# Prompt and memory attention between the K slabs, gates and memory caches between the V slabs: one decoder step on one core

## The reference

```python
q_sb, k_sb, v_sb, q_mem, p_rw, g_sb, g_mem, g_rw = _split(x @ w_in, IN_SPLITS)
o_sb = sb_mix(sb_heads(q_sb), k_sb, v_sb, sb_bias)        # stick-breaking attention, 8 heads of 64
o_mem = _mem_attend(q_mem..., mem_k, mem_v)               # softmax over 256 memory tokens, 4 heads of 128
o_rw, shift, wkv = _rwkv7(p_rw, ...)                      # a recurrence over the tokens, 8 heads of 64
merged = (jax.nn.sigmoid(g_sb) * (o_sb @ w_sb_o) + jax.nn.sigmoid(g_mem) * (o_mem @ w_mem_o)
          + jax.nn.sigmoid(g_rw) * (o_rw @ w_rw_o))
h = _layer_norm(DN_ALPHA * x + merged @ w_out, ln1_g, ln1_b)
y = _layer_norm(DN_ALPHA * h + _moe(h, ...), ln2_g, ln2_b)  # top 4 of 32 experts
```

## Time and profile before

| | us |
|---|---|
| median of 3 runs | 1773.66 |
| lowest, highest | 1770.39, 1776.94 |
| the profiled execution | 1772.1 |
| its span, first to last instruction | 1770.5 |
| TensorE busy | 1546.1 |
| VectorE busy | 596.5 |
| ScalarE busy | 278.0 |
| HBM read in MB | 528.65 |

### The profile page before, as it was taken

The page is one execution under the profiler, slowest core; times in us unless marked ns, Lnnn a source line. Parts: engine busy times, 40 slices in busy tenths (PEclk is TensorE's granted clock), DMA queues, the critical chain, the costliest instruction groups (busy, mean ns, idle before and its releaser), DMA issues.

```text
span 1770.5 us, 20938 instructions
## 1 busy us (share of the span) xinstructions
PE 1546.1 (87%) x7762; PEld 827.2 (47%) x7762; DVE 596.5 (34%) x888; ACT 278.0 (16%) x538; POOL 179.9 (10%) x285
## 2 busy tenths in 40 slices
PE   7976777768889997789999999999999999999992
PEld 5865534446777774444334343433343334334341
DVE  1699633157544445421212121111212121212125
ACT  1100233103311111201011101110111111011102
POOL 5422132102032112000000000000000000000000
PEclk9997878889989998889999999999999999999997
DMA  8798687765311105449999999999999999999970
GB/s 299 245 333 305 233 288 268 255 247 156 103 18 48 48 1 210 162 206 391 430 413 410 414 427 412 410 422 419 412 412 424 417 412 411 429 412 411 413 306 25
DMA packets 83769, 533.84 MB, mean 302 GB/s; under 512 B 8591, under 2 KB 9674, under 8 KB 59106
## 3 DMA queue, kind: packets, MB, share of 16 engines
q1 hardware_dynamic: 69714, 487.61, 68.1%
q0 software_dynamic: 14000, 45.53, 7.8%
HBM read 528.65 MB, written 4.46 MB: 301 GB/s over the span
## 4 chain that ended last, share of the span: by engine, by line
PE 78%; DVE 8%; issue 5%; ACT 4%; DMA 4%; POOL 1%; SPq 1%; POOLq 0%; DVEq 0%; ACTq 0%
PE bank L723 75%; PE bank L724 2%; DMA ring<-in_w_in 2%; ACT memT L1537 1%; ACT projT L1522 1%; DVE ring L1591 1%; DMA ring<-in_w_mem_kv 1%; DVE ring L1680 1%; DVE arena L1682 0%; DMA ring<-in_cache_sb_k 0%; DVE arena L1797 0%; DVE arena L1799 0%; DVE arena L1798 0%; ACT arena L1342 0%; DVE arena L2028 0%
## 5 line engine op out<-in xcount | busy, mean ns | idle before, releaser
L723 PE MATMUL bank<-arena 128*128 128x128 f32 (+9 forms) x2172 | 363.7, 357 | 38.0 <-DVE arena L1799 13.3
L723 PEld LDWEIGHTS bank<-arena 128*128 128x128 f32 (+3 forms) x2172 | 244.1, 184 | 165.2 <-issue 137.0
L723 PE MATMUL bank<-ring,memT 128*64 128x512 f32 (+2 forms) x1152 | 279.3, 598 | 43.3 <-ACT memT L1537 42.2
L723 PE MATMUL bank<-projT,ring 128*128 128x264 f32 x1056 | 265.1, 408 | 29.8 <-DMA ring<-in_w_in 20.9
L1968 DVE TENSOR_SCALAR arena<-bank 128x256 f32<-128x256 f32 x64 | 26.9, 420 | 689.9 <-PE bank L723 689.9
L723 PEld LDWEIGHTS bank<-projT,ring 128*128 128x128 f32 x1056 | 207.0, 201 | 76.9 <-issue 21.9
L723 PE MATMUL bank<-projT 128*64 128x512 f32 (+1 forms) x1056 | 231.2, 588 | 0.0
L723 PE MATMUL bank<-ring,projT 128*64 128x512 f32 x1024 | 228.7, 594 | 0.0
L723 PEld LDWEIGHTS bank<-ring,memT 128*64 128x64 f32 (+2 forms) x1152 | 86.7, 140 | 190.0 <-issue 133.9
L723 PEld LDWEIGHTS bank<-projT 128*64 128x64 f32 (+1 forms) x1056 | 78.1, 141 | 148.3 <-issue 147.7
L723 PEld LDWEIGHTS bank<-ring,projT 128*64 128x64 f32 x1024 | 72.2, 137 | 139.7 <-issue 139.7
(11 more groups left out here) (271 smaller groups left out, 979.0 us busy)
## 6 DMA issues: line engine op xcount, KB each, us to landing
ring<-in_w_gate_up SPq DMA_DIRECT2D x64, 2048.0 KB, 10.3
projT<-in_w_gate_up SPq DMA_DIRECT2D x64, 2048.0 KB, 13.1
ring<-in_w_down SPq DMA_DIRECT2D x64, 2048.0 KB, 10.2
ring<-in_w_in SPq DMA_DIRECT2D x13, 2048.0 KB, 9.2
ring<-in_cache_sb_k SPq DMA_DIRECT2D x64, 256.0 KB, 5.3
ring<-in_cache_sb_k POOLq DMA_DIRECT2D x64, 256.0 KB, 5.7
ring<-in_cache_sb_v SPq DMA_DIRECT2D x64, 256.0 KB, 4.8
ring<-in_cache_sb_v POOLq DMA_DIRECT2D x64, 256.0 KB, 5.1
```

The costliest lines, as they stand in the source:

```text
L723: mm = lambda out, l, r, first, last, **k: pe.matmul(out, l, r, start=first, stop=last, **k)
```

## The change

Prompt attention, memory attention, gates and caches get new places; what is computed stays the same. The new stream puts mkv 0 and 1 behind K4 and K6, ahead of win 4, and gate 0 ahead of K14 and K15. The samples' memory keys and gate 1 then alternate with pairs of V slabs, and mV 0 and 1 stand ahead of V12. The prompt's stick-breaking attention handles two head pairs (four heads) at a time, in buffers z4 and n4 of 4 x 384 columns. Its steps stand between projections on TensorE and one K slab apart on VectorE. Memory attention stands there too, with two sets of buffers, and ends behind the last projections, between gate tiles of branch 0. In the V stage each sample's memory query broadcast is followed by one gate tile of branch 1. Each gate tile is now moved out with the sigmoid itself, gate 1 into the merged buffer. A recurrence round has 18 branch steps instead of 22.

```diff
 def phase1_stream():
+    s = [win(0), key(0), win(1), key(1), win(2), key(2), key(3), win(3), key(4), ("mkv", 0), key(5), key(6), ("mkv", 1),
+         key(7), key(8), win(4), key(9), win(5), key(10), key(11), win(6), key(12), win(7), key(13), ("gate", 0, 0), key(14),
+         ("gate", 0, 1), key(15)]
+    s += [val(i) for i in range(4)] + [("mK", 0), ("gate", 1, 0)]
+    s += [val(i) for i in range(4, 8)] + [("mK", 1), ("gate", 1, 1)]
+    s += [val(i) for i in range(8, 12)] + [("mV", 0), ("mV", 1)] + [val(i) for i in range(12, 16)]
+    s += [("wo", 0), ("wo", 1), ("gate", 2, 0), ("gate", 2, 1), ("wo", 2), ("wout", 0), ("wout", 1)]
 def beside():
-    for kind, br in (("gate", 0), ("o", 0), ("gate", 1), ("o", 1), ("gate", 2)):
+    for kind, br in (("gate", 0), ("gate", 1), ("o", 0), ("o", 1), ("gate", 2)):
-GROUP_FIRST, GROUP_STEP = 160, 22
-PLACES = {"start": (0, 4), "X0": (4, 6), "X1": (6, 8), "X2": (8, 10), "X3": (10, 12), "X4": (12, 14),
-          "MV": (14, 16), "WT": (16, 18), "U0": (18, 20), "U1": (20, 22)}
+GROUP_FIRST, GROUP_STEP = 176, 18
+PLACES = {"start": (0, 2), "X0": (2, 4), "X1": (4, 6), "X2": (6, 8), "X3": (8, 10), "X4": (10, 12),
+          "MV": (12, 14), "WT": (14, 16), "U0": (16, 18), "U1": (18, 18)}
```

In psum_plan the projections turn over two banks instead of six:

```diff
+    p_banks = {ft: ft % 2 for ft in range(FT)}
+    p_banks.update({12: 0, 13: 1, 14: 4, 15: 5})
```

On TensorE:

```diff
+            project(8, 12)
+            query(2)
...
+            logits_pair(0)
+            project(12, 16)
+            query(3)
+            survive_pair(0)
...
+            query(4)
+            mem_values(0)
...
+            mix_pair(0)
+            logits_pair(1)
+            mem_values(1)
+            query(5)
+            project(16, 18)
...
+            survive_pair(1)
+            project(18, 22)
+            query(6)
+            project(22, 24)
+            mix_pair(1)
...
+            mem_logits(0)
+            mem_logits(1)
+            project(24, 27)
+            query(7)
+            project(27, FT)
+            mem_turn(0)
+            mem_turn(1)
+            mem_logits(2)
+            mem_logits(3)
+            branches(0, 8)
...
+            mem_mix(0)
+            mem_mix(1)
+            branches(8, 16)
+            mem_turn(2)
+            mem_turn(3)
+            branches(16, 24)
+            mem_mix(2)
+            mem_mix(3)
...
+            pe.wait_ge(sem("shift_cut"), 1)
...
+            branches(24, 56)
+            pe.wait_ge(sem("sp_s"), 1)
...
+            branches(56, 64)
+            sample_values(0)
+            sample_values(1)
+            sample_sum(0)
+            for bq in range(4):
                 q_broadcast(("mqb", bq), MQ0, NP_TOK + bq)
+                branches(64 + 8 * bq, 72 + 8 * bq)
+            sample_sum(1)
+            sample_values(2)
+            sample_values(3)
```

The later places of the branches on TensorE:

```diff
-            branches(64, 80)
+            branches(128, 144)
-            branches(80, 128)
+            branches(144, 160)
             over_heads("bon", T1, "rk_prod")
-            branches(128, 144)
+            branches(160, 168)
-            branches(144, 160)
+            branches(168, 176)
```

On VectorE:

```diff
+            key_slab(11)
+            mem_max(0)
+            mem_max(1)
+            key_slab(12)
+            mem_scale(0)
+            mem_scale(1)
+            mem_max(2)
+            mem_max(3)
+            key_slab(13)
+            mem_scale(2)
+            mem_scale(3)
+            key_slab(14)
             for ft in range(RW0, FT):
                 gone(v, ("p", ft))
             v.tensor_copy(psh[:], pT[:, RW0:FT, 255:T]).then_inc(sem("shift_cut"), 1)
+            key_slab(15)
```

On ScalarE:

```diff
+                    move(("gate", br, dt), gate_tile(br, dt), lambda b: b[:, 0:T], ACT.Sigmoid)
...
+            gate_moves(0, range(3, 7))
             act.wait_ge(sem("negabs_s"), 1)
             link(act.activation(sa_, sa_, ACT.Exp))
```

More of the change, by code:

```diff
@@ L104, in psum_plan, with project, query, logits @@
     add = lambda name, bank: g.append((name, bank))
+    fill = beside()
+    p_banks = {ft: ft % 2 for ft in range(FT)}
+    p_banks.update({12: 0, 13: 1, 14: 4, 15: 5})
+    def project(first, last):
+        for ft in range(first, last):
+            add(("p", ft), p_banks[ft])
+    def query(b):
+        add(("qb", b), 6 + b % 2)
+    def logits(pair):
+        for g4 in (2 * pair, 2 * pair + 1):
+            for hp in range(2):
+                add(("z", g4, hp), 2 + 2 * (g4 % 2) + hp)
+    def survive(pair):
+        for g4 in (2 * pair, 2 * pair + 1):
+            for hp in range(2):
+                add(("cs", g4, hp), 2 + 2 * (g4 % 2) + hp)
@@ L105, in psum_plan, with mix, gates, values @@
+    def mix(pair):
+        for g4 in (2 * pair, 2 * pair + 1):
+            add(("so", g4), 2 + g4 % 2)
+    def gates(first, last):
+        for i in range(first, last):
+            add(fill[i], i % 3)
+    def values(b):
+        add(("pv", b), 6 + b % 2)
     for k in range(KT):
         add(("xT", k), k)
[L107 to L116, removed]
@@ L117, in psum_plan @@
-    add(("qb", 7), 7)
-    for h in range(MH):
[L119 to L124, removed]
+    project(0, 4)
+    query(0)
+    query(1)
+    project(4, 8)
+    for k in range(KT):
+        add(("memT", k), 3 + k % 3)
+    add("params", 3)
+    add("shift_in", 4)
+    project(8, 12)
+    query(2)
+    for tt in range(3):
+        add(("kt", tt), (3, 5, 4)[tt])
+        add(("vt", tt), (4, 3, 5)[tt])
@@ L140, in psum_plan @@
-    for i, name in enumerate(beside()):
-        add(name, (3, 7)[i % 2])
[L142 to L155, removed]
+        add(("cs_s", i), 3 + i)
+    gates(7, 8)
+    values(0)
+    values(1)
@@ new lines, in psum_plan @@
+    add("so_s", 5)
+    for b in range(4):
+        add(("mqb", b), 4)
+        gates(8 + b, 9 + b)
+    values(2)
+    values(3)
+    for b in range(4, NB):
+        add(("mqb", b), 4)
+        gates(8 + b, 9 + b)
+    values(4)
+    add("mzT", 3)
+    values(5)
+    add("mpTs", 4)
+    add(("mpv", 0), 0)
+    add(("mpv", 1), 1)
+    values(6)
+    add("mo_s", 3)
+    values(7)
+    add("mo_sT", 2)
+    add("so_sT", 4)
+    for i, name in enumerate(fill[16:]):
+        add(name, (3, 7)[i % 2])
@@ new lines, in _ @@
+            for k in range(KT):
+                gone(pe, ("xT", k))
+            project(0, 4)
+            gone(pe, ("p", 3))
+            query(0)
+            query(1)
+            project(4, 8)
+            pe.wait_ge(sem("mem_in"), 16)
+            for k in range(KT):
+                b = start(("memT", k))
+                for tt in range(2):
+                    last = tr(b[:, tt * P:tt * P + P], memr[:, tt, k * P:(k + 1) * P])
+                done(("memT", k), last)
+            pe.wait_ge(sem("param_in"), 144)
@@ L1446, in _ @@
                 move(("kn", t), T2[:, t, :], lambda b: b[:, 0:T], ACT.Sqrt)
[L1447 to L1451 removed]
+            o_moves(0, range(4, KT))
             act.wait_ge(sem("cum"), 1)
@@ L1849, in _ @@
             v.sem_inc(sem("rw_done"), 2)
-            v.wait_ge(sem("gates_ready"), 3)
+            for dt in range(KT):
+                gone(v, ("gate", 2, dt))
             v.wait_ge(sem("branch_summed"), 16)
```

616 lines of the change are left out of this document (357 added, 259 removed).

## The result

The changed kernel took a median of 1794.99 us in four runs (1789.32 to 1796.98), the kernel before 1772.03 us beside it: a ratio of 1.0127, with a 95% interval of 1.0085 to 1.0168. Measured a second time later, with more runs of both, it was 1.0134 (1.0096 to 1.0173). So the kernel became slower by 1.3%, some 23 us. The forecast was 1780 us with a range of 1752 to 1803: the range held the time, the likeliest case (no measurable change, 0.43) did not happen, and slower had 0.35.

A forecast was written before the change was run, and what follows sets the result against it. Waits between TensorE, VectorE and the slab ring bound the first 400 us, TensorE the expert loop. From 1772.1 us, +42 - 30 - 4.1 - 1.6 gave 1778.6, as a median 1780; range 1752 to 1803.

The forecast's parts named there:

- Rival 2: V stage: gate 1 tiles run at 1.2 GHz, adding 29 us, 1804 us in all; chance 0.35 together with Rival 4.
- Rival 4: K stage: ScalarE's in-order waits leave projection banks full, stopping TensorE; 1792 us; chance 0.35 together with Rival 2.
- S: First matmul of the sample survival sums: 42 us later, at 263 us, between 242 and 275.
- S to M: Survival sums to VectorE's first token-shift subtraction: 150 us against 179.9, bounds 128 and 160.
- M to E: First token-shift subtraction to the expert loop: shorter by 4.1 and 1.6 us, as fewer branch steps stand there.
- TensorE's sum of 197 us: K stage: TensorE's work from 18.1 us until logits of memory heads 2 and 3 are there, at 215 us.
- The two dips of the queue: V stage: V loads wait for memory key slabs tied to gate tiles, leaving the DMA queue empty 8 and 9 us.
- The bon sums: Between kn and bon: 32 fewer branch steps, VectorE then sets the pace; 4.1 us gained of 15.
- GpSimd's four tiles: Branch 1 multiplications ahead of the wait for output states: about 7 us on an idle engine, cost 0.
- The rounds: Recurrence: four filling steps fewer in each of four rounds; 1.6 us gained in all, bounds 0 and 9.
- Rival 1: Ring slots come free early enough, the queue never runs dry, VectorE ends the K stage; 1750 us; chance 0.22.
- Rival 3: Recurrence is bound by TensorE, all 16 removed steps count: 7.5 us more gained, 1772 us; within the 0.43.

The follow-up runs named there:

- the pair of traces: Profiled executions of the changed kernel and of it with ScalarE's Exp and Ln for the sample logits ahead of its gate moves; the latter measured ratio 1.0059.
- the experiment: Changed kernel with the four memory query broadcasts ahead of the four gate tiles in both V stage groups, on two banks; ratio 1.0020.
- the three edits: Changed kernel with ScalarE's logits ahead of gate moves, memory query broadcasts ahead of gate tiles, and 22 filling steps a round; 1759.97 us, ratio 0.9924.

## Why the prediction was right or wrong

The range held 1795, and this is in part luck: its slower part was made for rivals 2 and 4, and neither brought the time. The error in S and that in S to M cancel, and the 15 us beyond the forecast came from M to E, where the sum forecast a gain.

**S, +42 predicted, +29.5 measured.** The term that failed is TensorE's sum of 197 us. Its work by then was 171 us, where the sum had 189 without its two allowances of 4 us: both pairs' logits took 3.9 us for 7, the survival sums 8.7 for 14, mixing and memory logits 7.0 for 10, and the memory keys 14.0 us for 17.0. The prediction called its rows full-clock rows, and they were not. This is the stretch of its row for the logits in the kernel before (columns as in the earlier trace rows, the clock third from the end), and then the logits of two head pairs in the changed kernel:

```profile
243.90:245.60 1.70, 1.70 (x14) 1.28 (x16) 0.00 (x0) 0.39 (x1) 0.76 (x2) 0.50 1.06 411
```

```profile
72.25 1.78 PE L787 MATMUL bank<-projT 64*128 64x256 f32 x16
```

The row of 8 logits records took 1.66 us at 0.50, and 16 records took 1.78 in the changed kernel; the survival row of 1.35 us stood at 0.62, the memory keys' row of 17.0 at 0.82. A price taken from a row whose granted clock is low is too high for a place where it is not. The idle time, 12 us for the 8 allowed, was mostly a wait of 6.67 us ahead of the first survival sums. So the logits were there at 201.3 instead of 215. The part behind it was right step by step: 49.1 us from there to S for 48, with K13 at once, VectorE idle for TensorE ahead of it (6.24 us, 9 or more had been named), the shift cut, four gate tiles, and ScalarE's Exp behind their sigmoids. ScalarE's order was counted in the sum, but its price was not seen as avoidable; it was 5 us in the pair of traces and 7 on average.

**S to M, -30 predicted, -17 measured.** The mechanism was right, the size of the first gap was off. The two dips of the queue were named, of 8 and 9 us; they measured 14 and 12, and V6's load went out at S+61.4 instead of S+52. Behind that the forecast had 98 us to M and 101.6 were measured. What the sum lacked is the four gate tiles themselves: their slab arrived at S+41.5 only, and from there four tiles and three broadcasts took 19.7 us, the first tile at a clock of 0.58 (6.39 us against 3.73). Rival 2 (the clock falls) was right for the first tile of each group, at 6.39 and 6.20 us, and wrong for the three others: 5 us, as the forecast had weighed it, and not 29. The idle times of 11 and 9 us ahead of the groups, which it had worked out, measured 10.30 and 9.71. Of the 16 us of low clock that the prediction reads as following an idle time in the kernel before, the first 4.8 lie within that idle time. That the interleaving ties the key slab's slot to gate tiles was seen; that untying it gives 11 to 17 us, the experiment showed.

**M to E, -5.7 predicted, +11.2 measured.** Three terms. The bon sums: 4.1 us gained was right in kind (3.1 in this execution, 3.1 to 6.2 in the others). GpSimd's four tiles "0, since it was idle then" was wrong: it was idle, but VectorE was not. Beside it three operations of VectorE took 1.76 us for 1.22 and the two x4 groups 7.7 for 5.0, which took the gain back, some 4 us. The rounds, 1.6 us gained with bounds of 0 and 9, was the step with the wrong sign: with fewer filling steps they took 6 to 12 us longer than before, and 8.0 us in the pair of kernels that differ in nothing else. From one round's first X product to the next it is 42.1, 45.9 and 43.3 us, where the prediction had named 41 to 42. The bounds should have reached below nothing: the sum priced the removed steps at what they take, and not at what they do for the clock of those that stay. In the two executions compared, M to X is 3.5 us longer, X to gm 5.8 and gm to E 2.0. This last part is not explained; it was 108.4 and 105.4 us in two executions of the same kernel.

**The rivals.** Rival 1 (queue never dry, 1750) did not occur; the three edits show that most of it was to be had. Rival 3 (rounds bound by TensorE's work, 1772) was refuted by the opposite sign. Rival 4 (TensorE stopped in the K stage by full banks behind ScalarE's order) did not occur: TensorE waited for ScalarE under 2 us there, and what ScalarE's order cost at S the sum had counted. The slower result came from mechanisms that stood in none of them: small amounts of matmul work taken out of a chain that waits, and GpSimd's work beside VectorE's.

What stays open: why S to M was also shorter in the kernel with ScalarE's logits first, so that its time fell by 12 us where 5 to 7 are explained, and what the low clock at the bon sums costs.

## What to carry to other kernels

When filler matmuls are moved out of a latency-bound chain, price the clock with them: here 16 of 88 steps fewer cost 8.0 us in that stretch and 0.4% of the time where nothing else was changed, and TensorE did less work in more time. When a price is read from a row, read the granted clock of that row too. When a buffer's release is tied by program order to work that waits for another load, put the work that frees it first. An engine that stands idle is not free because of that: GpSimd's tiles cost VectorE, which was on the path, some 4 us here.

## What the runs showed of the hardware

- With 22 and with 18 filling steps a round the mean granted clock over the four rounds was 0.97 and 0.90 in otherwise the same kernel, and they took 160.8 and 168.8 us. Over all executions 22 steps gave 0.94 to 0.97, 18 gave 0.87 to 0.90.
- VectorE's operations with two SBUF inputs went from 1.22 to 1.76 us (1024 columns) and from 2.49 to 4.67 us (four of 512) beside GpSimd's; GpSimd's from 0.74 to between 1.44 and 1.72 us.
- A gate tile behind 10.30 us of idle time took 6.39 us at a clock of 0.58, the next one, behind a broadcast, 3.73 at 1.00.
